# POOL's float32 subtractions issued as shorter instructions: weights in four pieces, attention logs in pieces of 448 columns

## The reference, cut to what matters

```
h = rmsnorm(x, norm_mix_g);  proj = h @ w_in            # 1024 x 7168: u_x, u_g, q, k, v, g_lru, g_att
y_lru = rg_lru(conv(u_x)) * gelu(u_g)
y_att = stick_breaking_attention(q, k, v)               # 16 heads, 4 blocks of 128 queries
        # log_1m = log_sigmoid(-z); suffix = reversed cumsum(log_1m); att = exp(log_sigmoid(z) + suffix)
x += (sigmoid(g_lru) * (y_lru @ w_br_lru) + sigmoid(g_att) * (y_att @ w_br_att)) @ w_out
x += square(relu(rmsnorm(x) @ w_mlp_up)) @ w_mlp_down   # width 4096
x += sigmoid(rmsnorm(x) @ w_ple_gate) * (p @ w_ple)
return rmsnorm(x)
```

## Time and profile before

| | us |
|---|---|
| median of the runs | 1737.38 |
| the profiled execution | 1737.41 |
| its span | 1735.6 |
| PE busy (matmul) | 1690.6 (97%) |
| DVE busy | 699.7 (40%) |
| ACT busy | 605.2 (35%) |
| POOL busy | 573.9 (33%) |

### The profile page before, as it was taken

One profiled execution on the slowest core, in us unless ns is written; L12 is line 12 of the kernel. 1 busy time (PEld: TensorE's weight loads), 2 busy tenths in 40 slices (PEclk: granted clock), 3 DMA queues, 4 the chain that ended last, 5 costly groups with the idle time before them and its releaser, 6 DMA issues.

```text
span 1735.6 us, 20034 instructions
## 1 busy us (share of the span) xinstructions
PE 1690.6 (97%) x8132; PEld 1172.3 (68%) x8132; DVE 699.7 (40%) x1124; ACT 605.2 (35%) x785; POOL 573.9 (33%) x276
## 2 busy tenths in 40 slices
PE   8999999999999999999999999999999999999996
PEld 5777766344434443537778877777788888888884
DVE  6766535233343333348651023333354421212246
ACT  5664444111000100124761255554333432323232
POOL 2331234222012202014334435554454444444441
PEclk9999999999999999999999999999999999999998
DMA  5221165899999999983222111112242222222301
GB/s 214 74 73 49 52 267 193 345 420 422 420 421 421 422 421 421 421 324 122 70 77 97 49 49 49 49 49 97 95 148 97 97 97 97 97 98 97 138 8 49
DMA packets 79068, 312.74 MB, mean 180 GB/s; under 512 B 3168, under 2 KB 6656, under 8 KB 54272
## 3 DMA queue, kind: packets, MB, share of 16 engines
q1 hardware_dynamic: 78704, 310.38, 45.8%
q0 software_dynamic: 272, 1.05, 0.2%
HBM read 307.22 MB, written 4.19 MB: 179 GB/s over the span
## 4 chain that ended last, share of the span: by engine, by line
PE 90%; DVE 6%; ACT 2%; issue 1%; POOL 1%; DMA 0%; DVEq 0%; SPq 0%; ACTq 0%
PE ps L915 44%; PE ps L1287 13%; PE ps L967 8%; PE ps L1311 7%; PE ps L1240 4%; PE ps L913 3%; PE ps L1437 2%; PE ps L1256 2%; PE ps L1257 1%; PE ps L1422 1%; PE ps L1480 1%; PE ps L1404 1%; DVE sb_xT L2364 1%; DVE sb_h_low L2083 1%; ACT sb_F L1530 0%
## 5 line engine op out<-in xcount | busy, mean ns | idle before, releaser
L847 POOL TENSOR_TENSOR sb_w_parts<-sb_slot,sb_w_parts 128x2048 fp32r<-128x2048 f32 x59 | 274.8, 4659 | 379.1 <-ACT sb_w_parts L1530 379.1
L915 PE MATMUL ps<-sb_h_high,sb_w_parts 128*128 128x512 f32 x1120 | 268.4, 392 | 0.0
L915 PEld LDWEIGHTS ps<-sb_h_high,sb_w_parts 128*128 128x128 f32 x1120 | 210.1, 188 | 47.0 <-issue 3.1
L1530 ACT ACTIVATE sb_w_parts<-sb_slot 128x2048 fp32r<-128x2048 f32 x59 | 112.7, 1913 | 195.7 <-PE ps L915 186.8
L1287 PE MATMUL ps<-sb_slot,sb_hT 128*64 128x512 f32 x768 | 171.1, 594 | 0.0
L915 PE MATMUL ps<-sb_hidden_high,sb_w_parts 128*128 128x512 f32 x704 | 165.0, 389 | 0.0
L915 PEld LDWEIGHTS ps<-sb_hidden_high,sb_w_parts 128*128 128x128 f32 x704 | 132.1, 188 | 27.5
L811 POOL TENSOR_TENSOR sb_tile_parts<-sb_slot,sb_tile_parts 128x1024 fp32r<-128x1024 f32 x32 | 77.9, 2435 | 184.7 <-ACT sb_tile_parts L1530 184.7
L915 PE MATMUL ps<-sb_h_low,sb_w_parts 128*128 128x512 f32 x560 | 138.0, 389 | 0.0
L1287 PEld LDWEIGHTS ps<-sb_slot,sb_hT 128*64 128x64 f32 x768 | 53.6, 137 | 106.2 <-issue 106.2
L833 POOL TENSOR_SCALAR sb_chosen<-sb_cst,sb_small 128x256 fp32r<-128x256 f32 x28 | 25.3, 921 | 293.5 <-PE ps L1240 293.5
(11 more groups left out here) (341 smaller groups left out, 2635.8 us busy)
## 6 DMA issues: line engine op xcount, KB each, us to landing
sb_slot<-w_up SPq DMA_DIRECT2D x24, 2048.0 KB, 14.6
sb_slot<-w_gate SPq DMA_DIRECT2D x24, 2048.0 KB, 14.5
sb_slot<-w_down SPq DMA_DIRECT2D x21, 2048.0 KB, 15.2
sb_slot<-w_in SPq DMA_DIRECT2D x14, 2048.0 KB, 7.9
sb_R<-w_down SPq DMA_DIRECT2D x11, 2048.0 KB, 15.2
sb_slot<-tiles SPq DMA_DIRECT2D x32, 512.0 KB, 3.3
sb_R<-w_gate SPq DMA_DIRECT2D x8, 2048.0 KB, 14.2
sb_R<-w_up SPq DMA_DIRECT2D x8, 2048.0 KB, 15.0
```

The source lines that it names most:

```text
L847: nc.gpsimd.tensor_tensor(low, raw_part(g), high.bitcast(F32), ALU.subtract).then_inc(w_low, 1)
L915: ins = nc.tensor.matmul(o, w[:, k, at:at + P], h[:, k, :], start=first, stop=last)
L1530: return nc.scalar.activation(dst, src, f, **kw)
```

## The change

In three places a POOL `tensor_tensor` subtraction is cut along its columns into several instructions that do the same arithmetic on the same data. Only the last of them counts up the semaphore, as the single one did.

- First block: 128x1024 becomes four of 128x256.
- Second block: 128x2048 becomes four of 128x512, and 128x1024 four of 128x256.
- Stick attention: 128x896 becomes two of 128x448; the 256 columns after it and the tail stay.

So 123 parts (32 at line 811, 59 of 2048 and 32 of 1024 columns at line 847) get three more instructions each, and 15 heads one more. The one part at line 838 stays whole. No other engine's program changes.

```diff
-                    nc.gpsimd.tensor_tensor(w1_parts[g % 2][1], raw1[g % SLOTS1], w1_parts[g % 2][0].bitcast(F32),
-                                            ALU.subtract).then_inc(w1_low, 1)
+                    for k in range(0, KD, 2):
+                        ins = nc.gpsimd.tensor_tensor(w1_parts[g % 2][1][:, k:k + 2, :], raw1[g % SLOTS1][:, k:k + 2, :],
+                                                      w1_parts[g % 2][0][:, k:k + 2, :].bitcast(F32), ALU.subtract)
+                    ins.then_inc(w1_low, 1)
...
-                nc.gpsimd.tensor_tensor(low, raw_part(g), high.bitcast(F32), ALU.subtract).then_inc(w_low, 1)
+                raw, n = raw_part(g), high.shape[1] // 4
+                for k in range(0, 4 * n, n):
+                    ins = nc.gpsimd.tensor_tensor(low[:, k:k + n, :], raw[:, k:k + n, :], high[:, k:k + n, :].bitcast(F32), ALU.subtract)
+                ins.then_inc(w_low, 1)
...
-                            for c, w_ in ((0, 896), (1024, 256)):
+                            for c, w_ in ((0, 448), (448, 448), (1024, 256)):
                                 ins = nc.gpsimd.tensor_tensor(Llow[h % 2][:, c:c + w_], Lb[h % 2][:, c:c + w_],
                                                               Lhigh[h % 2][:, c:c + w_].bitcast(F32), ALU.subtract)
```

## The result

The changed kernel takes **1743.2 us** (median of 9 executions, 1741.0 to 1744.7); the kernel before, run beside it, 1738.8 (median of 9, 1737.2 to 1740.6). The ratio is 1.0023 with a 95% interval of 1.0015 to 1.0032, which is +4.0 us (2.6 to 5.6). The forecast was +3.7. (Its absolute figure, 1741.1, stood on a time before of 1737.4, the median of three executions; with 1738.8 it would have been 1742.5.)

What follows compares the result with a forecast made beforehand. PE was taken to bound the kernel, with 90% of the chain that ended last. First block +0.4 and second block +3.3 gave +3.7 us on 1737.4, so 1741.1 us, range 1738.0 to 1743.0.

Steps and rivals of the forecast that it cites:

- The fixed cost: Every cut POOL part: a further piece costs 0.14 us (bounds 0.10 and 0.18), three more pieces 0.42.
- Tile 3, 808, 1203 and 1226: First-block tile 3, +0.4 us; second-block weight load at 808 us, +0.4; branch-product loads at 1203 and 1226, +0.8 together.
- The rival without overlap: All cut parts: pieces don't overlap, 0.18 us each instead of 0.14; +1.2 us, 1742.3; chance 0.10.
- ba2: Branch-product tile at 1249 us: DVE's product gets in during POOL's part, 0.42 + 0.47 = +0.9 us.
- the scan: First block's cumulative sum: DVE's scan starts sooner and PE gets all of the chain's gain, -1.2 us.
- POOL keeps the ports through its four pieces: Cut parts: DVE is not let in between pieces; sum +4.7 us, 1742.1; chance 0.08.
- short dispatch: Each POOL instruction: dispatch estimated at 0.04 us, fixed-cost terms under a third, sum about +1 us; not adopted.
- Start of the second block: Five queued DVE subtractions from 782.86 us: 0; the rival has DVE's gain reach the end, up to -1.2 here, chance 0.19.
- The signs: Trace marks: DVE low parts and scan under 2 us, given piece times, POOL busier, PE waiting longer for lines 811, 847.
- Seven odd heads: Stick-attention pairs: no slack between POOL's tail and PE's low pass, seven times 0.14, +1.0 us.
- Second tile: First block, near 19 us: three DVE sums of squares get in, POOL ends at 18.1, PE waits +0.8 us.
- 67.8 and 79.5: First-block weight loads at these times: the first hidden, 0 (+0.4 if cover is thin); the second in the chain, +0.4 us.

Runs made afterwards that it cites:

- the two signalled versions: h1_signal_no_logs and h2, measured at 1732.41 and 1732.54 us.
- h2: h1_signal_no_logs plus a signal after each POOL instruction for a stick-attention head, PE's low pass waiting one by one; 1732.54 us against 1738.58 before, ratio 0.9968.
- e7_selected: Kernel before with only three first-block tiles of line 811 (15, 19, 25) in four pieces; 1734.50 us against 1737.56, ratio 0.9981.
- h1_signal_no_logs: Kernel before with lines 811 and 847 in four pieces, each signalled and waited for by PE, logs whole; 1732.41 us against 1737.56, ratio 0.9965.

## Why the prediction was right, and where it was not

The time was right, with +3.7 forecast and +4.0 measured, and "slower, close to the edge of what can be told" was the likelier side. But the agreement of the sums is partly luck: the first block was put at +0.4 and is -1.4 in the steps (-0.8 in its own time, by the medians), the second at +3.3 and is +4.9 in the steps less 0.2 at its start (+2.7 and +2.0 in their own times). The two errors of -1.8 and +1.4 cancel.

**Right, by mechanism and size.**
- The fixed cost. Pieces were put at 1.29, 0.74 and 1.15 us and are 1.293, 0.737 and 1.157. In the pair above three instructions take 2.97 us where two took 2.81. Tile 3, 808, 1203 and 1226 show 0.37 to 0.45 for the 0.42. The rival without overlap falls.
- DVE gets in between pieces, and POOL then waits about 0.45: ba2 +0.88 for the +0.9 (0.42 + 0.47), the scan -1.3 for the -1.2. The rival "POOL keeps the ports through its four pieces" falls with it. So does the Trainium skill's short dispatch as a price (GPSIMD Engine Reference, 2.1): it would have made the terms a third. (The prediction puts the sum by that price at about +1 us; its own terms with 0.12 in the place of 0.42 and 0.04 in that of 0.14 give some +0.5.)
- Start of the second block: the step is -0.18 where 0 was forecast, and -1.2 was the rival's. That rival falls.
- MLP: 0.05, though DVE's longest low part went from 3.6 to 0.77 us. That gain lies beside PE.
- The signs: POOL's busy time +75.6 (at least 61 asked), the scan and the low parts under 2 us, PE's waits for POOL longer.

**Wrong.**
- *Seven odd heads, 7 x 0.14.* It measured 7 x 0.30. The step that failed is the sentence "DVE has nothing of two SBUF inputs at that time, so no hold". The instruction at that time is a cast with one input, and it is held too. I had counted the wrong class. The trace of before has it at zero slack (cast starting at 1044.78, POOL's end at 1044.93), and one cast of before, the second one, is held already, for POOL ends 0.30 after its start:

```profile
1024.42 0.99 DVE L2493 CAST sb_w_parts<-sb_slot 128x1280 fp32r<-128x1280 f32 x1
```

The Trainium skill (VectorE: DVE Perf Modes, What auto-detection actually checks) lets an instruction with a single source take the mode that uses both ports if source and destination lie in SBUF; it does not name casts, but by that rule this one belongs to it. The trace agrees: 1280 columns in 0.83 us, where two-input instructions take 0.69 for 512.
- *Second tile, +0.8.* It measured 0. The three holds were counted on top of a POOL time of 2.81 that held one already, and only two sums of squares fell into POOL's time after that. POOL took 3.73 us (13.52 to 17.25). PE's weight load, which comes ahead of its matmul, waited 0.20 for it (until 17.30), and the matmul due at 17.4 was not late.
- *The list of places was short.* The 2-column instruction at 158.9 (-0.95, the largest of the steps at places that were not on it), the steps at 59 (+0.1), 1195 (+0.34) and 1709 (+0.16). I searched for long DVE instructions and for PE's waits on POOL. A short instruction held for a microsecond on a chain that PE waits for shows in neither list; it shows as an instruction far above the others of its line or size.
- *67.8 and 79.5.* The 0.4 is paid at the first, which I called hidden, and not again at the second. One delay of a chain is paid where that chain first meets PE.

**What stays open.** Why the clock falls at just these places in some executions and not in others. Which of the two signalled versions is the faster. Why h2's pairs gain 0.13 instead of 0.05. Whether the three parts of e7_selected, cut alone and with a signal for each piece, would beat h1_signal_no_logs: no run has both.

## What to carry to other kernels

Shorter instructions on an engine that shares ports don't save or cost time as such: they give a microsecond where the other engine's chain ends in front of the bound engine, and cost a fixed 0.14 us each plus a hold for each instruction let in where their own end is awaited. So cut only the parts behind which a chain waits (three of 123 here: -3.3 us against +4.0 for all), and where a part is cut, signal each piece, so that whoever waits for the part can start. Look for the victims by how long they take for their size: a 2-column instruction of 1.4 us is the mark of such a wait.

## What the runs showed of the hardware that was not expected

- A DVE cast from SBUF to SBUF with one fp32 input (1280 columns, 0.83 us) is held up by POOL like an instruction with two inputs. It takes 0.83 alone and with POOL ending 0.15 after its start, 0.97 with POOL ending 0.29 after it, 1.12 with 0.44 (the second cast of the changed kernel). So is a scalar_tensor_tensor of 2 columns: the eight of line 2193 in before take 0.16 us with no POOL instruction beside them and up to 2.07 with one.
- With a queue on both sides the ports alternate instruction by instruction: POOL's four pieces of 256 columns take 4.75 us beside eight queued DVE subtractions; alone they would take 2.83, an estimate from the rows (4 x 0.737 less three overlaps of 0.04).
- Spells of TensorE at 1.2 GHz, eight matmuls long and worth up to 1.7 us, come at a few recurring places of the program in some executions only. Two traces of one kernel agree in their steps to 0.03 us, but for the start and the stretch from 765 to 790 us; in their totals they differ by up to 1.7 us for each spell that one has and the other has not.
